# A hybrid decoder layer on one core: PSUM banks dealt out differently between projections and transposes in the attention stage

## The reference

```python
xn = rms_norm(x, norm_mix_w[l])
proj = xn @ w_in[l]                      # b, c, h | q, k, v
yc = b * causal_depthwise_conv3(c * h)   # short form
# attention, per head and block of 128 queries, L keys up to the block's end:
z = jnp.einsum('bhqd,bhkd->bhqk', qb, kb) * scale
log_keep = jnp.where(mask, jax.nn.log_sigmoid(-z), 0.0)
suffix = lax.cumsum(shifted, axis=3, reverse=True)
A = jnp.where(mask, jnp.exp(jax.nn.log_sigmoid(z) + suffix), 0.0)
outs.append(jnp.einsum('bhqk,bhkd->bhqd', A, vb).astype(v.dtype))
x = x + jnp.concatenate([yc, ya], axis=-1) @ w_out[l]
x = x + hierarchical_moe(rms_norm(x, norm_ffn_w[l]), ...)
```

## Time and profile before

| what | us |
|---|---|
| median of 3 runs | 1212.92 (1211.42 to 1213.92) |
| profiled execution | 1212.0 |
| its span (first to last instruction) | 1210.3 |
| PE busy | 1108.4 (92% of the span) |
| DVE busy | 889.9 (74%) |
| ACT busy | 724.3 (60%) |

### The profile page before, as it was taken

How to read it: one execution, slowest core, us unless ns; L and a number is a source line. 1 busy time by engine, 2 the same in 40 slices (tenths; PEclk the granted TensorE clock), 3 DMA queues, 4 the chain that set the end, 5 groups by cost and what they waited for, 6 DMA issues and landing times. The chain is left out here.

```text
span 1210.3 us, 16764 instructions
## 1 busy us (share of the span) xinstructions
PE 1108.4 (92%) x5806; PEld 904.4 (75%) x5806; DVE 889.9 (74%) x993; ACT 724.3 (60%) x898; POOL 147.6 (12%) x196
## 2 busy tenths in 40 slices
PE   5998999999999959997699999999999999999960
PEld 4886777877778737886478888888888888888840
DVE  4404756566575565366689999999999999999946
ACT  5413554656733352113278888888888888888830
POOL 1001000010010042010110111111111011111000
PEclk9999999999999979999689999999999999999985
DMA  6201001101011144101799999999999999999619
GB/s 208 59 18 53 18 18 35 36 19 35 18 35 36 57 159 172 48 36 45 308 424 395 384 392 389 380 378 384 387 376 386 384 379 385 383 384 386 232 49 385
DMA packets 58380, 261.89 MB, mean 216 GB/s; under 512 B 14049, under 2 KB 34529, under 8 KB 45025
## 3 DMA queue, kind: packets, MB, share of 16 engines
q1 hardware_dynamic: 47968, 240.32, 51.9%
q0 software_dynamic: 9216, 16.80, 3.7%
q10 hardware_dynamic: 1152, 4.19, 0.8%
HBM read 252.89 MB, written 25.17 MB: 230 GB/s over the span
## 5 line engine op out<-in xcount | busy, mean ns | idle before, releaser
L996 DVE TENSOR_TENSOR e_lo<-W,e_hi 128x1024 fp32r<-128x1024 f32 x384 | 452.4, 1220 | 29.3 <-ACT e_hi L990 26.4
L990 ACT ACTIVATE e_hi<-W 128x1024 fp32r<-128x1024 f32 x384 | 403.1, 1060 | 100.6 <-PE ps L961 92.0
L959 PE MATMUL ps<-e_hi,xT_hi 128*128 128x512 f32 x512 | 204.9, 400 | 7.2 <-DVE e_lo L996 4.8
L961 PE MATMUL ps<-e_lo,xT_hi 128*128 128x512 f32 x512 | 201.6, 394 | 0.0
L960 PE MATMUL ps<-e_hi,xT_lo 128*128 128x512 f32 x512 | 201.3, 393 | 0.0
L746 DVE TENSOR_TENSOR_SCAN kept<-kept,start_at 128x1024 f32<-128x1024 f32 (+7 forms) x64 | 90.9, 1420 | 65.6 <-ACT kept L599 65.6
L419 PE MATMUL ps<-xnT_hi,w_hi 128*128 128x512 f32 x320 | 128.5, 401 | 2.4 <-DVE y_mix L721 0.9
L419 PE MATMUL ps<-xnT_hi,w_lo 128*128 128x512 f32 x320 | 128.1, 400 | 0.0
L419 PE MATMUL ps<-xnT_lo,w_hi 128*128 128x512 f32 x320 | 125.0, 391 | 0.0
L608 ACT ACTIVATE probsT<-ps 128x512 f32<-128x512 f32 (+3 forms) x96 | 43.8, 490 | 129.1 <-PE ps L468 128.9
L959 PEld LDWEIGHTS ps<-e_hi,xT_hi 128*128 128x128 f32 x512 | 97.8, 191 | 27.4 <-DVE e_lo L996 3.7
(11 more groups left out here) (217 smaller groups left out, 1677.2 us busy)
## 6 DMA issues: line engine op xcount, KB each, us to landing
W<-in_w_dram SPq DMA_DIRECT2D x96, 2048.0 KB, 10.9
w_raw<-in_w_in_dram SPq DMA_DIRECT2D x20, 512.0 KB, 4.0
yy<-y_rows SPq DMA_DIRECT2D x8, 1024.0 KB, 13.6
xt<-in_x_dram SPq DMA_DIRECT2D x8, 512.0 KB, 3.8
w_out_raw<-in_w_out_dram SPq DMA_DIRECT2D x4, 1024.0 KB, 8.1
xn_rows<-xn SPq DMA_DIRECT2D x8, 512.0 KB, 2.7
out_dram<-x ACTq DMA_DIRECT2D x8, 512.0 KB, 9.0
x<-in_x_dram SPq DMA_DIRECT2D x1, 3072.0 KB, 14.7
```

Source lines behind the costliest of these rows:

```text
L959: pe.matmul(o, xs_hi[:, k], e_hi[:, p, cols], start=(k == 0), stop=False)
L961: mm = pe.matmul(o, xs_hi[:, k], e_lo[:, p, cols], start=False, stop=(k == last))
L990: act.activation(e_hi[:, p], flat[:, p * D:(p + 1) * D], ACT.Copy).then_inc(s["hi_made"], 1)
L996: dve.tensor_tensor(e_lo[:, p], flat[:, p * D:(p + 1) * D], e_hi[:, p], ALU.subtract).then_inc(s["lo_made"], 1)
```

## The change

Groups from the ninth on use banks 5 and 7 in turns, by `group_bank`, and every group from the third on waits for the reading of the group two before it. The transposed halves all go to bank 4; every half from the second on waits for the copy of the half right before it, where it waited for the one two before. ACT's copy reads bank 4.

```diff
-        group_bank = lambda g: 6 + g % 2 if g < PRE_GROUPS else 7
+        group_bank = lambda g: 6 + g % 2 if g < PRE_GROUPS else 5 + 2 * (g % 2)
...
-        TB = lambda g: ps[:, 4 + g % 2]
+        TB = ps[:, 4]
...
-                            if PRE_GROUPS <= g:
-                                pe.wait_ge(bank_read[(g - 1) % 2], (g - 1) // 2 + 1)
-                            elif g >= 2:
+                            if g >= 2:
                                 pe.wait_ge(bank_read[g % 2], g // 2)
...
                         g = th(n, h) + hf
-                        if g >= 2:
-                            pe.wait_ge(turned_read, g - 1)
+                        if g:
+                            pe.wait_ge(turned_read, g)
                         for j in range(4 * hf, min(4 * hf + 4, length(n) // P)):
-                            mm = pe.transpose(TB(g)[:, (j % 4) * P:(j % 4 + 1) * P], soft[h][:, S - length(n) + j * P:S - length(n) + (j + 1) * P], ident)
+                            mm = pe.transpose(TB[:, (j % 4) * P:(j % 4 + 1) * P], soft[h][:, S - length(n) + j * P:S - length(n) + (j + 1) * P], ident)
...
-                        act.activation(probsT[h][:, k0:k1, :], TB(th(n, h) + hf)[:, 0:(k1 - k0) * P].rearrange("p (k t) -> p k t", t=P),
+                        act.activation(probsT[h][:, k0:k1, :], TB[:, 0:(k1 - k0) * P].rearrange("p (k t) -> p k t", t=P),
                                        ACT.Copy).then_inc(turned_read, 1)
```

## The result

| | before | after |
|---|---|---|
| median, us | 1213.06 (4 runs) | 1237.22 (1236.01 to 1239.91, 4 runs) |
| ratio | | 1.0204 (95%: 1.0191 to 1.0216) |
| profiled execution, us | 1212.0 | 1236.0 |
| its span, us | 1210.3 | 1234.3 |

The account below looks back on a forecast made before the run. TensorE's in-order queue was taken as the bound, 285.27 of 288.00 us busy. 28.8 + 0.3 - 2.7 - 1.3 - 0.5 = 24.6 us on 1212.0 gave 1236.6, as median 1237.5 us; range 1230 to 1246.

Parts of the forecast that it names:

- One stall, 0.90 us, 32 times: Attention, units of two halves: fifth transpose waits for ScalarE's copy of the first four, 0.90 us, 32 times, 28.8 us.
- The prediction's sign for it: Row for 130 to 418 us some 24 us longer, same busy time; about 32 waits for the copy, 20 to 29 us.
- The prediction's list of waits: TensorE's waits before: projections' largest 0.9 us; 4.7, 4.2 and 2.6 us before values and scores, outside the 288 us.
- Turns of one half cost nothing: Turns of 4 tiles or fewer fit one bank; projections or the values step already cover their copy wait, so no cost.
- The bank waits of projections, 4.0 us, each beside a stall: Second projection bank returns 2.7 us at starts of pairs 1 to 3 and 1.3 us in the last pair.
- ScalarE late, 0.3 us: In the unit of 8 opening pairs 1 and 2, ScalarE's lateness costs 0.15 us twice, 0.3 us.
- The rival of a late ScalarE: Units of 8 and 7 tiles lose 4 us more, with upper-bound stalls: 33 us, 1246 us; chance 0.06.
- The last units, 0: Last four units, without projections: head 1's turn waits for head 0's copy, but counted 0, at most 0.5 us.
- Unit 0, 0.5 us returned: Unit 0: a stall in head 0's turn comes out of head 1's 0.51 us wait for VectorE, 0.5 us back.
- The clock, in the steady part: Rival: stalls drop the clock to 1.2 GHz for a tenth of the 288 us, 14 us more, 1252 us; chance 0.03.

Follow-up runs that it names:

- The filled gaps: Changed kernel with 2 or 4 projection matmuls moved between the two halves of a turn: 1224.01 us with 2, 1212.81 us with 4.
- The run with one stall: Kernel before with one added wait, in unit 0's first turn the second half waiting for the first's copy: 1216.37 us in one run.
- VectorE's early reading: Kernel before, with VectorE reading a pair's last projection group ahead of the next unit's weighing for head 1: 1210.39 us, ratio 0.9978.
- the transposes' half alone: Kernel before with one bank for the transposes only, projections staying in bank 7 with the old wait: 1238.31 us, ratio 1.0211.
- filled stalls and one projection bank: Changed kernel with 4 projection matmuls between a turn's halves, but projections in bank 7 with the old wait: 1219.22 us, ratio 1.0053.
- two banks in the last units: Changed kernel with filled stalls, 10 and 14 matmuls, reordered sigmoids, and transposes using banks 4 and 5 in the last four units: 1209.61 us, 0.9974.

## Why the prediction was right

The whole was 0.3 us off, in part by luck. Of its 24.6 us, 23.0 belong to the steady part (30 stalls of 0.90 less the 4.0 of the projections; ScalarE's 0.3 would make it 23.3), which grew by 22.96 us. Unit 0 was wrong by 1.1 us, and the chance difference of the two traces outside the stage, 1.5 us, covered it. By its steps:

- **One stall, 0.90 us, 32 times.** Right in each term. From one unit of two halves to the next the trace after falls behind by two stalls: values steps that stood at 209.00, 219.28 and 228.82 us stand at 217.47, 229.56 and 240.94, so the lag grows from 8.47 to 10.28 and 12.12, 0.91 us for a stall. The prediction's sign for it, some 24 us more with the same busy time and 32 waits, came out as 24 us (288 to 312) with 5.07 us more of busy time (285.27 to 290.34) and 32 waits of 0.69 us, 22.1 us in all: the profile counts part of each stall as busy. The filled gaps show that the stall is a plain wait, and the kernel with only the wait changed shows that the bank has no price of its own. The prediction's list of waits left out the line of transposes waiting for VectorE, 4.1 us in four waits, of which the longest is 3.0; all four stand at 123.58, 128.18, 426.10 and 443.40, outside the 288 us, so its reading holds.
- **Turns of one half cost nothing.** Right: from unit 4 to unit 7 of pair 0 the lag stays at 7.54 to 7.55 us (values steps at 174.87 and 182.41; 199.07 and 206.62).
- **The bank waits of projections, 4.0 us, each beside a stall.** Right in size and place, and so was the remark that the stall covers the reading: the old wait, kept, costs 0.34 us beside it. "Returned" was the wrong word for the sum, though: the 4.0 us are not earned by the second bank, they are the part of the 28.8 us that falls where TensorE would have stood anyway. The rule on rotating banks (the Trainium skill, Perfetto Trace Analysis, section Matmuls) got its test both ways: taken from the transposes it cost 24 us, until other work of the queue filled the gap; given to the projections it was worth 0.3 us here and 6.5 us once the stalls were filled. The trace agrees with it only where nothing else on the queue covers the reading.
- **ScalarE late, 0.3 us.** Right that it is small. In the turn shown above, ScalarE ran without idle time into head 1's first copy (211.32), which still starts 0.64 us after the first transpose, and in the same turn of pair 2 it is 0.63; so not even the 0.15 us were lost, twice. The rival of a late ScalarE was dead for this kernel, and became true once the stalls were filled.
- **The last units, 0.** Right: from the turn of unit 28 to the last turn it took 23.65 us before (419.75 to 443.40) and 23.72 after (444.79 to 468.51). The 2.6 us wait shrank to 1.7 in exchange for 0.78 in the turn, and the copy of unit 30 held TensorE 3.9 us where the values step had waited before.
- **Unit 0, 0.5 us returned.** Wrong in sign. From the first turn to unit 0's values step it took 10.54 us before and 12.97 after (123.22 to 136.19): 2.4 us for two stalls of 0.9, so 0.6 us lost beyond the two stalls where 0.5 were to be returned, 1.1 us apart. The 0.5 us of waiting for VectorE did go: head 1's turn starts at 129.34 without a wait. But the step left out that a stall at the low clock puts off the clock's return, so that the projections behind it run slowly for longer. The trace after has the clock at 0.50 for over 3 us longer:

```profile
123.00:126.00 3.00, 2.14 (x11) 1.70 (x10) 3.00 (x3) 0.60 (x1) 0.00 (x0) 0.50 0.00 0
126.00:129.00 3.00, 3.00 (x9) 2.32 (x9) 2.97 (x3) 2.39 (x3) 0.00 (x0) 0.50 0.00 0
129.00:132.00 3.00, 2.31 (x14) 1.76 (x13) 1.81 (x2) 1.18 (x3) 0.00 (x0) 0.91 0.00 0
```

  against, before,

```profile
126.00:129.00 3.00, 2.49 (x15) 1.84 (x15) 2.96 (x3) 2.11 (x4) 0.00 (x0) 1.00 0.00 0
```

  The run with one stall, and the twelve traces side by side, show that the stall does it. With it the stage lost 25.5 us, not 24.6. That the total still fitted is luck: it is owed to 1.5 us outside the stage, which lie within what those stretches vary by.
- **The clock, in the steady part.** Not lowered: 130 to 442 us has 290.34 us of TensorE work in 312 us at 1.00, with 31 of the 32 stalls in it.

```profile
130.00:442.00 312.00, 290.34 (x1852) 223.36 (x1852) 175.25 (x172) 158.22 (x265) 19.39 (x17) 1.00 0.08 24
```

  The Trainium skill's account of a clock that goes up and down when TensorE idles briefly between PSUM groups (TensorE: Matmul & The Clock Gate, section on psum-queue depth-cycling) isn't borne out by waits of 0.69 us at the high clock. It is told of another kernel, in bf16, without the length of its gaps, so the two need not contradict each other. It is at the low clock that such a wait mattered here.

## What to carry to other kernels

Where one engine's queue is the path, a buffer given back one step later costs, at each use, the whole handover there and back (here 0.64 + 0.60 + 0.05 + 0.05 us, from the first transpose on) less the time that the queue would have worked before the refill anyway (0.44 us); count the uses, and read the four numbers from rows that are already in the trace. A second buffer earns only what the rows show as wait, and nothing at a place where another wait already stands. Before asking for more PSUM, look whether work already on the queue can stand between filling and refilling: four matmuls moved into the gap returned what the lost bank had cost, and then the next engine's order of work and the matmuls' shares decided the rest. And where the time of an execution varies by more than the effect, compare a stretch between two fixed steps in two traces: here such stretches agree to 0.01 us where the order of work is the same.

## What the runs showed of the hardware

**A short wait delays the clock's return.** After the wait of 4.2 us TensorE's work began again at 120.81 us in the kernel before and the granted clock was back at 1.00 by 126; with one stall of 0.69 us in between, work began at 121.63 and 130 us had passed before it was back. Over all traces it is 4.6 to 6.0 us without such a stall and 8.4 to 9.1 with it. At 2.4 GHz the same stall left the clock alone, in each of the 30 stalls of units 1 to 27.

**In the last units the clock falls early in some traces and not in others**, with nearly the same waits. The kernel with only the wait changed, and the changed kernel, in the same 5 us:

```profile
450.00:455.00 5.00, 4.33 (x16) 2.49 (x14) 2.91 (x4) 3.12 (x8) 4.90 (x5) 0.50 1.01 408
```

```profile
450.00:455.00 5.00, 4.33 (x18) 2.03 (x14) 4.47 (x4) 4.28 (x9) 5.00 (x5) 1.00 0.98 392
```

From unit 28's values step to unit 29's the first took 11.24 us and the second 9.10. The waits just ahead are the same in both (1.68 us for take_values, then 0.67). Five of the six kernels with filled stalls, the one with VectorE's early reading and the one with one stall had a fall by then as well (9.40 to 11.24 us); the kernel before, the changed one, the one with the transposes' half alone and the one with filled stalls and one projection bank had not (9.02 to 9.11). What decides it is open; taking the short waits away (two banks in the last units) did not prevent it, at 0.66 in 420 to 425 us. Nor do these single traces show that it belongs to a kernel: of 61 executions of the kernel before, the ten with a mean granted clock of 0.964 or 0.965 took 1207.75 to 1210.23 us, and the fifty-one at 0.958 to 0.961 took 1210.45 to 1214.94. So up to 2 us of any single trace of this stage are the clock's, and that is the size of the differences among the fastest versions.
